# Two quarter blocks of weights per transfer in a two-layer diffusion backbone on one core

## The reference

```python
# layer 0: attention with 8 heads and a gated short convolution, side by side
pl = modulate(x, norm_mix_g[0], sh1, sc1) @ ev_w_in            # 2048 -> 4608
mix_l = concat([latent_attention(q_l, k_l, v_l, k_c, v_c), short_conv_mixer(...)])
x = x + g1 * (mix_l @ ev_w_out)                                # 2048 -> 2048
# layer 1: Hyena long convolution over the tokens
p = depthwise_conv(modulate(x, ...) @ od_w_in, conv_w) + conv_b   # 2048 -> 6144
x0, x1, v = split(p); y = x0 * bidir_long_conv(x1 * v, filt, skip)
x = x + g1 * (y @ od_w_out)                                    # 2048 -> 2048
# both layers
x = x + g2 * (square(relu(modulate(x, ...) @ ffn_w1)) @ ffn_w2)   # 2048 -> 8192 -> 2048
# the shifts, scales and gates: silu(c) @ mod_w[l], 2048 -> 12288 for each layer
```

## Time and profile before

| | us |
|---|---|
| median of 3 executions | 2548.94 |
| lowest and highest | 2548.2, 2550.98 |
| the profiled execution: its own time | 2554.98 |
| the profiled execution: span in the trace | 2553.2 |
| PE busy in it | 2437.0 |
| DVE busy | 1812.1 |
| ACT busy | 957.9 |

### The profile page before, as it was taken

How to read it: one execution, slowest core, us unless ns; L and a number is a source line. 1 busy time by engine, 2 the same in 40 slices (tenths; PEclk the granted TensorE clock), 3 DMA queues, 4 the chain that set the end, 5 groups by cost and what they waited for, 6 DMA issues and landing times.

```text
span 2553.2 us, 48068 instructions
## 1 busy us (share of the span) xinstructions
PE 2437.0 (95%) x19008; PEld 2310.8 (91%) x19008; DVE 1812.1 (71%) x2651; ACT 957.9 (38%) x959; POOL 0.2 (0%) x4
## 2 busy tenths in 40 slices
PE   6899799998999999999999999999999999999997
PEld 2379489998999999999999989999999999999997
DVE  3557669988888877878878777875877555555555
ACT  4433333334334333334433223223443333333333
POOL 0000000000000000000000000000000000000000
PEclk7789899999999999999999999999999999999998
DMA  9887079986888887888875565556677555555552
GB/s 347 278 321 264 1 281 342 334 318 220 304 291 291 299 301 258 300 300 293 290 274 179 190 247 199 204 190 213 219 284 252 185 184 182 166 182 182 182 182 99
DMA packets 266080, 614.39 MB, mean 241 GB/s; under 512 B 12208, under 2 KB 12336, under 8 KB 265456
## 3 DMA queue, kind: packets, MB, share of 16 engines
q1 hardware_dynamic: 260992, 602.08, 67.8%
q10 hardware_dynamic: 4912, 9.77, 1.1%
HBM read 605.51 MB, written 6.29 MB: 240 GB/s over the span
## 4 chain that ended last, share of the span: by engine, by line
PE 86%; DVE 6%; DMA 3%; ACT 2%; issue 1%; SPq 0%; DVEq 0%; ACTq 0%
PE acc L515 78%; PE aux L612 1%; ACT w_hi L1326 1%; DMA w_raw<-mod_first 1%; PE aux L782 1%; PE aux L803 1%; DMA w_raw<-od_w_in 1%; DMA scr<-k_freq 1%; PE aux L512 1%; DVE w_lo L837 1%; PE acc L623 1%; DVE summed L969 1%; PE acc L738 1%; DVE m_raw L845 1%; DVE act_a L974 0%
## 5 line engine op out<-in xcount | busy, mean ns | idle before, releaser
L837 DVE TENSOR_TENSOR w_lo<-w_raw,w_hi 128x2048 fp32r<-128x2048 f32 x372 | 851.3, 2289 | 474.5 <-ACT w_hi L1326 459.4
L1326 ACT ACTIVATE w_hi<-w_raw 128x2048 fp32r<-128x2048 f32 x372 | 711.8, 1915 | 1216.1 <-PE acc L515 1151.3
L515 PE MATMUL acc<-act_a,w_hi 128*128 128x256 f32 x6784 | 881.0, 286 | 24.1 <-issue 12.8
L515 PEld LDWEIGHTS acc<-act_a,w_hi 128*128 128x128 f32 x6784 | 850.9, 195 | 31.3 <-issue 20.9
L515 PE MATMUL acc<-act_b,w_hi 128*128 128x256 f32 x5120 | 645.0, 284 | 3.6 <-DVE summed L877 2.4
L515 PEld LDWEIGHTS acc<-act_b,w_hi 128*128 128x128 f32 x5120 | 628.1, 192 | 5.5 <-DVE summed L877 2.6
L515 PE MATMUL acc<-act_a,w_lo 128*128 128x256 f32 x3392 | 448.7, 283 | 0.0
L515 PEld LDWEIGHTS acc<-act_a,w_lo 128*128 128x128 f32 x3392 | 426.4, 192 | 0.0
L515 PE MATMUL acc<-act_b,w_lo 128*128 128x256 f32 x2560 | 335.2, 283 | 0.0
L515 PEld LDWEIGHTS acc<-act_b,w_lo 128*128 128x128 f32 x2560 | 319.6, 192 | 0.0
L845 DVE SCALAR_TENSOR_TENSOR m_raw<-m_raw,wide 128x1024 f32<-128x1024 f32 x176 | 212.0, 1218 | 9.0 <-issue 9.0
(11 more groups left out here) (140 smaller groups left out, 906.2 us busy)
## 6 DMA issues: line engine op xcount, KB each, us to landing
w_raw<-ffn_w SPq DMA_DIRECT2D x256, 1024.0 KB, 6.8
m_raw<-mod_rest SPq DMA_DIRECT2D x176, 512.0 KB, 5.6
scr<-mod_rest SPq DMA_DIRECT2D x144, 512.0 KB, 5.9
w_raw<-od_w_in SPq DMA_DIRECT2D x48, 1024.0 KB, 7.8
w_raw<-ev_w_in SPq DMA_DIRECT2D x36, 1024.0 KB, 8.6
w_raw<-mod_first SPq DMA_DIRECT2D x32, 1024.0 KB, 9.5
w_raw<-ev_w_out SPq DMA_DIRECT2D x16, 1024.0 KB, 8.5
w_raw<-od_w_out SPq DMA_DIRECT2D x16, 1024.0 KB, 5.2
```

Source lines behind the costliest of these rows:

```text
L515: return pe.matmul(acc[ft][:, 0:T], w, rhs[:, k, a:a + T], start=start, stop=stop)
L837: TT(w_lo[:, kg % 2, :], w_raw[:, kg, :], w_hi[:, kg % 2, :].bitcast(F32), ALU.subtract)\
L1326: return act.activation(out_, in_, func, **kw)
```

## The change

The four transfers of a unit become two. `half_block` brings quarters 0 and 1, or 2 and 3, in one transfer of 2 MB. It counts on `landed[0]` or `landed[2]`, and `hi` waits for that one for both quarters. The wait before the first transfer is now for lo(u-1, 1), before the second for lo(u-1, 3). The tiles between are grouped: all four of `before` behind the first transfer, all of `own` behind the second. The block of unit 3 that is written out by hand gets the same form; there all four of its own tiles now stand behind the wait for `o_full`, where two stood ahead of it. `mod_block` is as it was.

```diff
+            def half_block(h, w, row, col):
+                sp.dma_start(w_raw[:, 2 * h:2 * h + 2, :].rearrange("p k (c n) -> p (k c) n", c=4),
+                             w[ds(row + h * 1024, 1024), ds(col, 512)].rearrange("(c p) n -> p c n", p=P))\
+                    .then_inc(landed[2 * h], 16)
...
-                for kg in range(4):
+                for h in range(2):
                     if first:
-                        raw_free(START, kg)
+                        raw_free(START, 2 * h)
+                        raw_free(START, 2 * h + 1)
                     else:
-                        sp.wait_ge(lo_done, (u - 1) * 4 + (kg + 1))
-                    sp.dma_start(w_raw[:, kg, :].rearrange("p (c n) -> p c n", c=4),
-                                 w[ds(row + kg * 512, 512), ds(col, 512)].rearrange("(c p) n -> p c n", p=P))\
-                        .then_inc(landed[kg], 16)
-                    if kg < 2:
-                        mod_tiles(before[2 * kg + 4:2 * kg + 6], old or slots)
+                        sp.wait_ge(lo_done, (u - 1) * 4 + (2 * h + 2))
+                    half_block(h, w, row, col)
+                    if h == 0:
+                        mod_tiles(before[4:8], old or slots)
                     else:
-                        mod_tiles(own[2 * kg - 4:2 * kg - 2], slots)
+                        mod_tiles(own[0:4], slots)
...
-            for kg in range(4):
-                sp.wait_ge(lo_done, (U_CONV - 1) * 4 + (kg + 1))
...
-                if kg < 2:
-                    mod_tiles(mods(2)[2 * kg + 4:2 * kg + 6], EARLY)
+            for h in range(2):
+                sp.wait_ge(lo_done, (U_CONV - 1) * 4 + (2 * h + 2))
+                half_block(h, ev_w_in, 0, KV_HI + 2 * CONV_W)
+                if h == 0:
+                    mod_tiles(mods(2)[4:8], EARLY)
                 else:
-                    if kg == 3:
-                        sp.wait_ge(o_full, N_Q)
-                    mod_tiles(mods(3)[2 * kg - 4:2 * kg - 2], WIDE)
+                    sp.wait_ge(o_full, N_Q)
+                    mod_tiles(mods(3)[0:4], WIDE)
...
-                act.wait_ge(landed[kg], u * 16 + (16 * START + 16))
+                act.wait_ge(landed[kg // 2 * 2], u * 16 + (16 * START + 16))
```

More of the change, by code:

```diff
@@ L442, in conv_unit @@
                      mods(j * 3 + (3 + n)), mods(j * 3 + (2 + n)), old=old)
-            for kg in range(4):
-                sp.wait_ge(lo_done, (U_CONV - 1) * 4 + (kg + 1))
-                sp.dma_start(w_raw[:, kg, :].rearrange("p (c n) -> p c n", c=4),
-                             ev_w_in[kg * 512:kg * 512 + 512, KV_HI + 2 * CONV_W:KV_HI + 2 * CONV_W + 512]
-                             .rearrange("(c p) n -> p c n", p=P)).then_inc(landed[kg], 16)
-                if kg < 2:
-                    mod_tiles(mods(2)[2 * kg + 4:2 * kg + 6], EARLY)
-                else:
-                    if kg == 3:
-                        sp.wait_ge(o_full, N_Q)
-                    mod_tiles(mods(3)[2 * kg - 4:2 * kg - 2], WIDE)
+            for h in range(2):
[3 more added lines that the diff above has]
+                    mod_tiles(mods(2)[4:8], EARLY)
+                else:
+                    sp.wait_ge(o_full, N_Q)
+                    mod_tiles(mods(3)[0:4], WIDE)
             conv_unit(0, 1)
```

## The result

The changed kernel takes 2585.92 us in the median of four runs (2577.36 to 2590.59), the kernel before 2548.57 beside it (2546.5 to 2550.98): a ratio of 1.0143, with a 95% interval of 1.0125 to 1.0162. It is slower, as forecast. The time lies 13.9 us above the 2572.0 forecast and 0.1 us inside the upper end of the range. The profiled execution took 2586.69, its span is 2584.9: 31.7 longer than before's. The medians are 37.4 apart, because before's profiled execution lay 6 us above its median and this one only 0.8. So the traces have to explain 31.7.

A forecast was written before the change was run, and what follows sets the result against it. The prediction took PE, busy 95% of the span, as the bound. Hyena stage 19.4, start 2.2 and after the attention 1.5 sum to 23.1 us on the median 2548.94, giving 2572.0 us, range 2556 to 2586.

The forecast's parts named there:

- The bound and the chain: Hyena stage: B's last tile holds SP's queue, delaying C's weights; each microsecond the landing slips is one for PE.
- The second MB, four times 2.7: Start of four Hyena units C: `hi(C,0)` must wait for 2 MB, 2.7 us later each, 10.8 us in all.
- The clock, four times 1.7: After PE's longer idle time before units C, the clock falls to half speed: 1.7 us each, 6.8 in all.
- Units A let through 1.8: Hyena units A: weights slip 2.7 us, DVE reaches its product late; 1.8 us comes through to PE at the inverse.
- the 19.4 of the sum: Whole Hyena stage: second transfer half 10.8, clock 6.8 and units A 1.8 us make 19.4 us.
- The start, 2.2: Unit 0: the first pair must wait for the second step of `mod_rows`, costing 2.2 us (0.9 to 3.5).
- After the attention, 1.5: Units 3 and 4: all four tiles of unit 3 issued after the attention delay unit 4, 1.5 us (0 to 2.4).
- Everywhere else, nothing: All other units, MLPs included: the later 2 MB transfers stay hidden with 2 to 4 us of slack, costing nothing.
- The second rival: Losses smaller than the sum, as the second MB comes almost with the first: 2551 to 2560 us, chance 0.14.
- the third: Faster: leaner transfers bring the late copies before units 6 and 9 in time, no Hyena loss: 2541 us, chance 0.04.
- the fifth: No change: the pair lands in front of C as fast as today, leaving 2.2 + 1.5 us at the edges; chance 0.06.
- The fourth: Cover gone in tile-full stages: half blocks late in some 40 units, 2610 to 2630 us, or a few, 2585 to 2600; chance 0.12.

The follow-up runs named there:

- pair_before_tile: Changed kernel, 2 MB everywhere; in the Hyena stage the last tile of units B and C is issued behind the next unit's first pair: 2555.74 us, 1.0023.
- hyena_four: Changed kernel with units 45 to 57 (Hyena stage and the unit behind) back to four transfers, old waits and order: 2564.01 us, 1.0066.
- edges_four: Changed kernel with unit 0 in quarters and tiles 0 and 1 of unit 3 ahead of the wait for `o_full`: 2572.95 us, 1.0095.
- all_three: Changed kernel with units 0 and 45 to 57 in quarters, and tiles 0 and 1 of unit 3 ahead of the wait for `o_full`: 2554.10 us, 1.0017.
- order_only: Changed kernel's order and waits, but each pair is two 1 MB transfers and `hi` waits for its own quarter: 2555.13 us, 1.0029.
- old_at_loop: Changed kernel's order with 1 MB transfers, but units 14, 22, 30 and 38 back to the old order and waits: 2554.99 us, 1.0025.
- weights_first: Kernel before, 1 MB transfers; in the Hyena stage the last tile of units B and C moved behind the next unit's quarters 0 and 1: 2542.77 us, 0.9977.

## Why the prediction was right, and where it was small

**The bound and the chain: right.** Most of the loss sits where the forecast put it, behind the last tile of unit B, and `pair_before_tile` shows that this place is its cause: take the tile away from in front of the pair and 2 MB costs nothing there.

**The second MB, four times 2.7: right.** `hi(C,0)` starts 9.50, 9.01, 9.08 and 9.18 us after the issue in the four blocks (9.0 to 9.5 named), before 6.77, 6.80, 7.09 and 6.51. PE's idle time before the four units C is 3.20, 3.12, 3.19 and 3.29 us (3 to 3.9 named), and the starts of these units slip by 2.73, 2.21, 1.99 and 2.68: 9.6 us for the 10.8 of the sum, and in each block what the landing slipped by, so "every microsecond is one for PE" holds to the letter. A transfer alone takes 3.0 us more than one of half its size, but behind a tile the difference is 2.4 in the mean of the four. The estimate by the Trainium skill was 2.4 for the second MB ("DMA: Bandwidth & Descriptors", section "Anatomy of one DMA"), from a fit for the GpSimd path; of the two rows here for SP's transfers one agrees and one lies above it.

**The clock, four times 1.7: right.** It falls behind each of the four idle times, to 0.52 for 3.4 us, and the units behind slip by 1.47, 1.49, 1.29 and 1.49: 5.7 for 6.8.

**Units A let through 1.8: near in number, not shown as a cause.** What is left of the stage is 18.1 - 9.6 - 5.7 = 2.8 us, and it comes at the inverse in the last two blocks (1.57 and 1.65 us), where PE waits 1.71 and 1.57. But the last of these steps is there without any pair too (1.3 to 1.9 us at unit 58 in the four other kernels with quarters in the stage and the tile in its old place). PE's waits before the four inverses add up to 2.1 us in before, to 3.4 to 4.3 in those four, and to 4.0, 4.8 and 5.5 in the three traces with pairs behind the tile. About 1 us of this term is thus the pairs', and that the number came out near is partly luck. DVE's waits for `k_freq` have shrunk to one, but it is in the last block, where the forecast had none left: that the slack is used up block by block, from 2.1 us down, was not what happened. The second half block of unit B is used right behind its landing, 0.16 us, in three of the four blocks, and ACT waits for it 0.1 to 0.2 us longer than it would for PE (4.00 us below, where waits for PE are 3.84). So pricing it at nothing was right with no margin left.

```profile
1480.26 1.92 ACT L1328 ACTIVATE w_hi<-w_raw 128x2048 fp32r<-128x2048 f32 x1 [4.00 <-DMA w_raw<-od_w_in]
```

The stage as a whole, for the 19.4 of the sum: 18.1 and 19.9 in the two traces, and 19.2 in the medians of `hyena_four`.

**The start, 2.2: the term was too small.** The table has 6.7 and 7.1 in the two traces of this kernel and 3.5 and 4.2 in two others with the same start, but the steps of `mod_rows` ahead of it do not end at the same time in all traces. Counted from the end of the last of them, `hi(0,0)` starts after 0.56 us in all six traces with quarters at unit 0 and after 5.2 to 5.6 in the four with a pair: 4.9 us in the mean. With the fall of the clock behind it unit 1 starts 5.7 to 6.1 us later, and the 10.2 us of `edges_four` less 3.9 for units 4 and 5 leave 6.3. What was too small is the transfer: the forecast took 7.8 us and up to 2.6 for the stores, and in the middle of its bounds 9.1. It was 11.8, where a pair alone takes 8.1; that the stores beside it make the other 3.7 is likely and was not tested. The forecast rightly counted the whole pair, as `hi(0,0)` can use nothing of the first MB before the second has landed. The semaphore's count is why: by the Trainium skill, "DMA: Bandwidth & Descriptors", section "Why a DMA increments its semaphore by 16 and not by 1", only the full 16 means that the data is there. The trace agrees: `hi(0,0)` starts at 156.64, as all of the pair has landed. The fall of the clock behind 5.99 us of idle PE, 0.9 us by unit 1, was counted in the Hyena stage and not here.

**After the attention, 1.5: too small by 2.4.** It measured 3.9, and the order alone 4.0, so the size of the transfers plays no part. The pair of unit 4 was to have landed 15.9 us behind the issue of the first tile (350.5 less 334.58); `hi(4,0)` starts 17.8 us behind it (360.28 less 342.48). That is the late case that the forecast had bounded, at 2.4, and unit 4 slips by 2.47. But the pair does not set the time: with the order alone `hi(4,0)` waits for PE, and unit 4 slips by 2.55 all the same. The tile behind it does, for which DVE waits in both (2.74 and 2.77 us), until 19.0 us behind the first tile's issue. A fall of the clock behind PE's idle time was left out here too: it is the 1.45 us of unit 5.

**Everywhere else, nothing: failed in the first MLP.** From unit 6 to 46 it was 3.0 and 3.4 us. The steps at units 22, 23 and 29 took 1.5, 1.0 and 1.4, and unit 10 gave 1.3 back: PE waits 2.36 us before unit 9 in before and 2.37 here, and the clock fell behind it in before only. The forecast named ACT waiting for `ffn_w` as what would prove it wrong; this it does in the first MLP, 10.9 us in four waits, and never in the second. In most units the 2 to 4 us of slack are there. The step that failed was to read the slack from units in the middle of the loops, and to take 7.8 us and a tile or two for the transfer there. At a turn DVE stands still, and what it does late releases the next transfers late and in a bunch. The timeline from 789 to 830: SP issues a pair at 789.10, and DVE stands still until 797.44, 3.1 us longer than before. The next pair goes out at 804.40, four tiles behind it, and at 813.57 the first pair of unit 23, as soon as its slots are free. It lands 13.6 us later, and ACT waits 5.21 us for it.

```profile
789.10 0.38 SPq L400 DMA_DIRECT2D w_raw<-ffn_w  x1
...
797.44 1.23 DVE L847 SCALAR_TENSOR_TENSOR m_raw<-m_raw,wide 128x1024 f32<-128x1024 f32 x1 [6.80 <-issue]
...
804.40 0.38 SPq L400 DMA_DIRECT2D w_raw<-ffn_w  x1
...
813.57 0.38 SPq L400 DMA_DIRECT2D w_raw<-ffn_w  x1
...
827.29 1.92 ACT L1328 ACTIVATE w_hi<-w_raw 128x2048 fp32r<-128x2048 f32 x1 [5.21 <-DMA w_raw<-ffn_w]
```

`all_three` shows that such a rest exists (1.0017, above 1); `order_only` and `old_at_loop` have no such waits for `ffn_w`, so these waits take both the late release and the 2 MB. The steps have different causes. That at unit 22 comes before any of these waits: PE waits 1.36 us for DVE's copies, which the longer standstill made late, and `order_only` has it too (1.45). That at unit 23 needs the late pair. That at unit 29 is neither: PE itself stands still there with no cause that the trace shows, 3.87 us in before, 5.22 here, 4.5 to 6.0 in seven of the other traces and not at all in that of `weights_first`; whether the change lengthens it stays open. How much of the 4.6 us each has was not separated.

**The sum and the rivals.** Forecast 23.1, traced 31.7: Hyena 1.3 less, the start 4.5 more, after the attention 2.4 more, between them 1.2 at units 2 and 3, the rest 1.7 more. Of the start's 4.5 some 0.6 is `mod_rows` ending later. The 1.2 come in all four traces with a pair at unit 0 (1.1 to 1.2): the clock falls there once more, for 3.4 us behind a wait of PE of 1.9 to 2.0 us in the attention, and behind the same wait in none of the six others; why only then stays open. That is 8.5 of the miss of 13.9. The other 5.4 us are not a term: the forecast moved the median by the same sum as the profiled execution, and this kernel's profiled execution fell near its median while before's had been 6 above. That the time is still inside the range, by 0.1 us, is luck; the direction is not, nor is the Hyena stage, 18.1 us for 19.4. The second rival (smaller losses), the third (faster) and the fifth (no change) fall with the measured 9.0 us and the four falls of clock; PE's waits before units 6 and 9 are also what they were, 2.4 us each. The fourth (cover gone) is true of one or two units of the first MLP and for 1 to 2 us, not for the stages full of tiles.

## What to carry to other kernels

When transfers are merged, ask of each consumer when its first byte is usable, not how many bytes a second come: where a transfer's issue is allowed long before but stands in an in-order queue behind another that waits, every microsecond of the larger transfer is one for the bound engine. Look for that queue first. Moving one small transfer behind the weights was worth 27 us here with 2 MB and 6.7 us with 1 MB. And where a new idle time of PE is forecast, count the slower clock behind it at every such place, at the edges of the kernel too, but as a chance and not as a certainty: behind PE's wait of 2.4 us before unit 9 it fell in two of ten traces.

## What the runs showed of the hardware

DVE's standstill at the turn of its loop depends on what SP issues at that point. In the seven traces with two quarters or a pair issued at that point it was 6.1 to 7.4 us (14 of 14), in the three with the old order there 3.1 to 5.3 (6 of 6). The busy times of that stretch show the traffic beside it: DVE does nothing, and 302 GB/s move in the changed kernel (first row), 147 in the one before (second).

```profile
790.70:797.40 6.70, 6.70 (x58) 6.70 (x57) 0.00 (x0) 2.85 (x2) 0.00 (x0) 1.00 0.87 302
```
```profile
779.60:783.20 3.60, 3.60 (x32) 3.60 (x32) 0.00 (x0) 0.99 (x1) 0.00 (x0) 1.00 0.39 147
```

The trace names nothing that DVE waits for, but it holds a trail. Some DMA packets are on queues that the profile calls "instruction"; the changed kernel has 40 on queue 14 in its whole span. The queues of that stretch, 790.7 to 797.4:

```profile
q14 instruction: 2, 0.02, 0.6%
```

In each of the 20 standstills, in all ten traces, exactly two packets of 8 KB start on queue 14, and DVE runs again 1.7 to 1.8 us after the second has ended, whether it stood still for 3.1 us or for 7.4. The second starts 0.7 to 2.7 us into the standstill in the three traces with the old order and 4.1 to 5.4 us in the seven others. So DVE's restart follows these packets, and the packets come later with two quarters or a pair issued just ahead; that the traffic of the weights is what holds them up is argued from these times and not shown.

The clock does not answer to the length of an idle time alone. Behind 2.36 to 2.39 us of idle PE before unit 6 it fell in nine of the ten traces; behind the same wait before unit 9 in two of the ten; and in `order_only` it fell behind 1.77 us.

A 2 MB transfer beside four stores of 256 KB took 11.4 to 11.8 us in four traces, 3.3 to 3.7 more than alone. In the first MLP, behind a pair and four tiles, one took 13.6 us.
